# Woven stationary weights: two 128-column tiles side by side, element by element

## What is computed

```python
for l in range(DEPTH):                                   # first_block
    h = rms_norm(x, g_mix[l])
    proj = h @ w_in[l]                                   # 1024 x 10052, split into branch inputs and gates
    ...
    merged = gates[0] * (ya @ w_oa) + gates[1] * (yb @ w_ob) + gates[2] * (yc @ w_oc) + gates[3] * (yd @ w_od)
    x = x + merged @ w_merge[l]
    h2 = rms_norm(x, g_ffn[l])
    gt = causal_dwconv(h2 @ w_ffn_gate[l], ffn_conv_w[l])
    x = x + (silu(gt) * (h2 @ w_ffn_up[l])) @ w_ffn_down[l]
for l in range(DEPTH):                                   # second_block
    proj = rmsnorm(x, norm_w[l]) @ w_in[l]
    ...
    x = x + concat([y_mla, y_gdn, y_moba]) @ w_out[l]
```

## Time and profile before

| what | value |
|---|---|
| median of the runs shown (2: 1377.38 and 1378.05) | 1377.72 us |
| span of the profiled execution, first to last instruction | 1369.2 us |
| median less that span | 8.5 us |
| TensorE, matmuls busy / weight loads busy | 1345.0 / 1265.4 us |
| VectorE busy | 1040.0 us |
| ScalarE busy | 750.9 us |
| mean granted TensorE clock | 0.996 of full speed |

### The profile page before, as it was taken

How to read it: one execution, slowest core, us unless ns; L and a number is a source line. 1 busy time by engine, 2 the same in 40 slices (tenths; PEclk the granted TensorE clock), 3 DMA queues, 4 the chain that set the end, 5 groups by cost and what they waited for, 6 DMA issues and landing times. The chain is left out here.

```text
span 1369.2 us, 26498 instructions
## 1 busy us (share of the span) xinstructions
PE 1345.0 (98%) x10828; PEld 1265.4 (92%) x10828; DVE 1040.0 (76%) x1781; ACT 750.9 (55%) x1157; POOL 46.3 (3%) x48
## 2 busy tenths in 40 slices
PE   8999999999999999999999999999999999999998
PEld 8899999998999989899999999999989899888996
DVE  6999898677766666999897767766778746777565
ACT  6544656556444455544557545544558546576363
POOL 0000000000000000000000000000000110001100
PEclk9999999999999999999999999999999999999999
DMA  8565444564665465645364555555553324353231
GB/s 289 177 207 178 131 154 160 180 215 155 197 202 185 139 230 163 215 155 185 97 204 159 187 187 172 198 185 191 178 186 124 120 64 137 100 174 109 78 102 69
DMA packets 108992, 223.77 MB, mean 163 GB/s; under 512 B 6180, under 2 KB 17700, under 8 KB 108872
## 3 DMA queue, kind: packets, MB, share of 16 engines
q1 hardware_dynamic: 106736, 219.12, 48.2%
q10 hardware_dynamic: 2136, 2.96, 0.7%
HBM read 221.01 MB, written 1.06 MB: 162 GB/s over the span
## 5 line engine op out<-in xcount | busy, mean ns | idle before, releaser
L1755 DVE TENSOR_TENSOR wlo<-ring,whi 128x1024 fp32r<-128x1024 f32 (+3 forms) x430 | 498.1, 1180 | 182.7 <-ACT whi L1173 152.7
L1173 ACT ACTIVATE whi<-ring 128x1024 fp32r<-128x1024 f32 (+3 forms) x430 | 433.2, 1026 | 361.8 <-PE bank L499 228.7
L499 PE MATMUL bank<-hhi,whi 128*128 128x256 f32 x2016 | 278.8, 280 | 6.0 <-ACT sgb L1431 3.9
L508 PE MATMUL bank<-hhi,wlo 128*128 128x256 f32 x2016 | 280.3, 281 | 0.0
L499 PE MATMUL bank<-hlo,whi 128*128 128x256 f32 x2016 | 275.3, 278 | 0.0
L499 PEld LDWEIGHTS bank<-hhi,whi 128*128 128x128 f32 x2016 | 253.1, 189 | 9.5 <-ACT sgb L1431 4.3
L508 PEld LDWEIGHTS bank<-hhi,wlo 128*128 128x128 f32 x2016 | 252.6, 189 | 3.7 <-issue 2.6
L499 PEld LDWEIGHTS bank<-hlo,whi 128*128 128x128 f32 x2016 | 251.6, 189 | 0.0
L469 PE MATMUL bank<-w 64*64 64x64 f32 (+5 forms) x1376 | 101.7, 249 | 1.5 <-DMA w<-in_flip 0.9
L1935 DVE SCALAR_TENSOR_TENSOR w<-w,par 128x256 f32<-128x256 f32 x240 | 98.0, 478 | 0.0
L521 PE MATMUL bank<-whi,hhi 128*128 128x512 f32 (+2 forms) x256 | 96.6, 379 | 0.0
(11 more groups left out here) (309 smaller groups left out, 1535.5 us busy)
## 6 DMA issues: line engine op xcount, KB each, us to landing
ring<-in_w_in SPq DMA_DIRECT2D x100, 1024.0 KB, 5.1
ring<-in_w_ffn_down SPq DMA_DIRECT2D x22, 1024.0 KB, 5.1
ring<-in_w_ffn_gate SPq DMA_DIRECT2D x20, 1024.0 KB, 5.1
ring<-in_w_ffn_up SPq DMA_DIRECT2D x20, 1024.0 KB, 5.1
ring<-in_w_merge SPq DMA_DIRECT2D x8, 1024.0 KB, 5.1
ring<-in_w_out SPq DMA_DIRECT2D x8, 1024.0 KB, 5.0
ring<-in_w_oc SPq DMA_DIRECT2D x4, 1024.0 KB, 5.3
ring<-in_w_od SPq DMA_DIRECT2D x4, 1024.0 KB, 5.2
```

The lines of the kernel that those rows point to most:

```text
L499: done = e.matmul(o, wh[:, k, cols(u)], s_[:, k0 + k, :], stop=False, skip_group_check=True, start=opens and k == 0 and s_ is sh and u % 2 ...
L508: done = e.matmul(o, wl[:, k, cols(u)], sh[:, k0 + k, :], start=False, stop=closes, skip_group_check=True)
L1173: e.activation(part_of(whi, j), part_raw(j), ACT.Copy).then_inc(*up("hi.a"))
L1755: e.tensor_tensor(part_of(wlo, j), part_raw(j), part_of(whi, j), ALU.subtract).then_inc(*up("lo.v"))
```

## The change

Parts that `chans` uses are marked `woven`. In whi and wlo their columns are stored in pairs of tiles: for each k-row and each pair q of 128-column tiles, element i of the first tile, then element i of the second, and so on. Both splits write in this order (VectorE also reads whi in it) and read the ring as before. `chans` takes tile u as member u % 2 of pair u // 2, so its stationary operand has a step of two elements, 8 bytes. Parts for moving operands, `ba` and `cvg` stay as they were.

```diff
-        def load_k8(w, c0, c1):
+        def load_k8(w, c0, c1, weave=True):
...
-                load_k8(w, c0, c0 + (512 if n == 4 else n))
+                load_k8(w, c0, c0 + (512 if n == 4 else n), kind == "chans")
...
-                    load_k8(w, c0, c1)
+                    load_k8(w, c0, c1, name not in ("m0", "cvg"))
...
+        def weave_of(buf, j):
+            return part_of(buf, j).rearrange("p k (q i s) -> p (k q) s i", s=2, i=P)
+
+        def split_of(buf, j):
+            return weave_of(buf, j) if woven[j] else part_of(buf, j)
+
+        def split_raw(j):
+            raw = part_raw(j)
+            return raw.rearrange("p k (q s i) -> p (k q) s i", s=2, i=P) if woven[j] else raw
...
-                wh, wl = part_of(whi, j), part_of(wlo, j)
+                wh, wl = weave_of(whi, j), weave_of(wlo, j)
...
-                            done = e.matmul(o, wh[:, k, cols(u)], s_[:, k0 + k, :], stop=False, skip_group_check=True,
+                            done = e.matmul(o, wh[:, k * nq + u // 2, u % 2], s_[:, k0 + k, :], stop=False, skip_group_check=True,
...
-                        done = e.matmul(o, wl[:, k, cols(u)], sh[:, k0 + k, :], start=False, stop=closes,
+                        done = e.matmul(o, wl[:, k * nq + u // 2, u % 2], sh[:, k0 + k, :], start=False, stop=closes,
...
-                e.activation(part_of(whi, j), part_raw(j), ACT.Copy).then_inc(*up("hi.a"))
+                e.activation(split_of(whi, j), split_raw(j), ACT.Copy).then_inc(*up("hi.a"))
...
-                e.tensor_tensor(part_of(wlo, j), part_raw(j), part_of(whi, j), ALU.subtract).then_inc(*up("lo.v"))
+                e.tensor_tensor(split_of(wlo, j), split_raw(j), split_of(whi, j), ALU.subtract).then_inc(*up("lo.v"))
```

More of the change, by code:

```diff
@@ L378, in build, with load @@
         mask1 = cst[:, zo:zo + S]
-        loads, parts = [], []
-        def load(src, cuts):
+        loads, parts, woven = [], [], []
+        def load(src, cuts, weave=False):
             for c in cuts:
                 parts.append((len(loads),) + c)
+                woven.append(weave)
             assert src.shape[1] * src.shape[2] <= SLOT
             loads.append((src, src.shape[1], src.shape[2]))
-        def load_k8(w, c0, c1):
+        def load_k8(w, c0, c1, weave=True):
             for k in (0, 4):
-                load(w[:, k:k + 4, c0:c1], [(0, 2, 0, c1 - c0), (2, 4, 0, c1 - c0)])
+                load(w[:, k:k + 4, c0:c1], [(0, 2, 0, c1 - c0), (2, 4, 0, c1 - c0)], weave)
         def load_wide(w, k):
@@ L401, in build @@
             w = by_k(a["w_in"][l])
-            for _, _, n, c0 in MIX_IN:
-                load_k8(w, c0, c0 + (512 if n == 4 else n))
+            for _, kind, n, c0 in MIX_IN:
+                load_k8(w, c0, c0 + (512 if n == 4 else n), kind == "chans")
             for _, bi, name, _ in BRANCHES:
@@ L408, in build @@
                     load_k8(w, c0, c0 + 512)
-                    load(wo[:, :, 512 * hf:512 * hf + 512], [(0, 2, 0, 512), (2, 4, 0, 512)])
+                    load(wo[:, :, 512 * hf:512 * hf + 512], [(0, 2, 0, 512), (2, 4, 0, 512)], True)
             for i in range(4):
@@ L484, in chans @@
             def chans(j, held, n, src, k0, opens, closes, mid=None, normed=None):
-                wh, wl = part_of(whi, j), part_of(wlo, j)
+                wh, wl = weave_of(whi, j), weave_of(wlo, j)
                 sh, sl = src
-                kn = wh.shape[1]
+                kn, nq = 2, n // 2
                 e.wait_ge(SEM["hi.a"], j + 1)
```

## The result

| | before | after |
|---|---|---|
| median of the runs | 1377.72 us | 1402.74 us (2 runs, 1402.15 and 1403.34) |
| span of the profiled execution | 1369.2 us | 1400.4 us |
| ratio after / before | | 1.0189, 95% interval 1.0163 to 1.0215 |

Slower, by 25.0 us in the medians and 31.2 us in the spans. The forecast was 1369 us, with a range up to 1398. The two differences are unlike because the span of before lies 8.5 us under its median and that of after 2.3 us under its own. Every other kernel's profiled execution took 1.7 to 1.9 us more than its span, so the profiled execution of before took about 1371 us (an estimate) and was faster than either of the two in the table. On the chips of the experiments, where the kernel before ran beside the others, its medians are 1371.65 to 1373.67; against those the change costs 29 to 31 us.

The account below looks back on a forecast made before the run. TensorE was taken as the bound, number of products times their distance. Loads -9 us and splits zero took the span from 1369.2 to 1360, and the median from 1377.7 to 1368.7, say 1369 us; range 1334 to 1398.

Parts of the forecast that it names:

- What bounds the kernel: TensorE, busy 1345.0 of 1369.2 us with waits of at most 3.9 us: number of products times their start-to-start distance.
- The floor: For 256-column products, 113.3 ns is the moving columns streaming by themselves, not the loading of 128 columns.
- Loads: TensorE's loads of woven tiles: the longer distance goes away across 6816 products, taken as 9 us saved.
- the longer distance: 117.7 ns between 256-column products in the mixing stage against 113.3 in feed-forward; the 4.4 ns surplus comes once per tile loaded.
- the third: Rival on TensorE's loads: woven loads touch twice the memory lines and always meet the stream; +17 us, 1395; chance 0.11.
- its mark: Expected timeline sign of the third: all groups of eight at 1.10 us and weight loads longer than 0.19 us.
- The first rival: TensorE's two distances are a phase that the load's step does not touch; nothing moves, 1377.7 us; chance 0.24.
- The two rules: Trainium skill passages: by the read-port one time stays 1377.7; by the cacheline one neither splits nor loads pay anything.
- Splits: ScalarE's whi and VectorE's wlo writes (1063 and 1226 ns): taken as zero change, at most a doubling, +1.07 us each.
- The size of the verdict: Whole-kernel chances against a 2% threshold, 27.6 us: faster 0.15, slower 0.11, within 0.74.

Follow-up runs that it names:

- the bench: Separate kernel without the reference's computation: sets of 64 back-to-back products varying load step, moving width and tile size; 256 columns with full unit-step tiles took 120.0 ns by the starts.
- e2_writes: Kernel after, with woven writes kept but stationary tiles loaded at unit step; median 1374.01 us, ratio 1.0011 to the kernel before.
- e9_unit_112: Kernel before, with both weight buffers moved up 80 bytes, so tokens lie 112 bytes past weights modulo 256; 1404.80 us, ratio 1.0237 to the kernel before.
- e10_woven_80: Kernel after, with both weight buffers moved up 112 bytes, so tokens lie 80 bytes past weights modulo 256; 1417.83 us, ratio 1.0334 to the kernel before.

## Why the prediction was wrong, step by step

- **What bounds the kernel** held: the number of products times their distance, with no wait in between. The whole change of time is a change of that distance.
- **The floor** held: 113.3 ns is the 256 moving columns (32-column tiles at unit step: (7.4 - 0.277) / 63 = 113.1). The 8-column tiles of the bench have 113.6 at an 8-byte step and, for no reason that a run shows, 116.7 at unit step, both by the starts.
- **The step that failed is the term "Loads", -9 us.** It measured +31 us. I took the surplus of the longer distance to be a meeting of load and stream (the runs bear that out: it comes and goes with the addresses of the two, and with the size of the tile), and then let a step of 8 bytes take it away, on no more than that the order of the load changes. In place of it the runs showed two things. The stepped load takes longer by itself, 117.8 ns against 111.5, because it touches 64 lines of 16 bytes and not 32; no product can follow the last sooner than that, which is at least (117.8 - 115.2) x 6816 = +17.7 us. And a stepped load holds up the stream more than one of unit step does, also where it has time to spare (233.4 against 227.1 ns with 512 moving columns). In the kernel the distance is 120.0, (120.0 - 117.8) x 6816 = +15 us above the load alone. The sum, 32.7, is the span's growth within 1.5 us, but the two parts are an accounting: no run has the one without the other in the kernel.
- **The rivals.** The right one was the third, "every woven load touches twice the memory lines", at a chance of 0.11. Half of its mark was there (loads longer than 0.19 us, no group at 1.07; but the groups read 1.12 and not 1.10), and it was priced with the longest distance that the trace had, 117.7, so it gave +17 and 1395 where +31 was due. The step that mis-sized it is "even a load 5% slower would put every product at 117.7 or so": a load 5.6% slower puts it at 120 at these addresses. The range ended at 1398 because of that. A distance that no row shows can lie beyond the longest that rows show.
- **The first rival**, that the two distances are a phase which the step does not touch, is half right: at one set of addresses and unit step both exist (192 bytes in the table). But the step does touch it.
- **The two rules.** The Trainium skill, "TensorE: Matmul & The Clock Gate", the step on loading the stationary operand in Part 2, has two independent read ports and so no change. The runs disagree: 64 bytes of padding between the operands' buffers turn 113.3 or 117.7 into 120.0 ns with unit steps in both, and beside a stepped load the stream of 512 columns slows from 227.1 to 233.4. The Trainium skill, "SBUF — State Buffer", Door 1, the note on cachelines, says that two accesses per 16-byte line keep full bandwidth. The runs confirm the 16-byte line and nearly the rule: one and a third accesses per line cost 175.6 ns, one 233.4, two 117.8. But two are not quite four, 117.8 against 111.5, and in a kernel whose loads have 1 ns of room that is at least half of the loss. For the moving operand the rule fails by a factor of two: at two accesses per line 256 columns take 230 ns.
- **Splits** held: zero on VectorE (1226 to 1228 ns), and the 69 ns more on ScalarE lie in its idle time, as e2_writes shows (+0.1%). The last sentence of that part has the order reversed: the splits run up to four parts ahead of TensorE, not TensorE ahead of them. Nothing hung on it, since no split grew where it counted.
- **The size of the verdict.** The chances gave 0.11 to slower by over 2%; the result is 1.9% with an interval of 1.6 to 2.2, so these runs do not say on which side of the 2% it lies; that it is slower they do say.

What stays open: what in the two addresses decides (the difference modulo 256 bytes counts; e9_unit_112 and e10_woven_80 show that it is not all, and whether the rest is the place of the weights within 64 bytes was not tested by itself), how a stepped load holds up the stream, and what switches the kernel before between 113.3 and 117.7 with unchanged operands.

## What to carry to other kernels

Where loads of stationary tiles and the stream of moving columns are nearly as long as each other, keep both at unit step: with two elements in each 16-byte line instead of four a load took 6% longer here, with one it took twice as long. When buffers are moved, added or padded, look at the start distances of the products again, since an allocation that has nothing to do with them can change them by 6%. And try a layout change at more than one start of the other operand: the weaving cost some 29 us with the tokens 192 bytes past the weights, and against unit steps at 0 bytes it cost nothing.

## What was not expected of the hardware

- A load of 128 float32r elements per partition goes by 16-byte lines, about 1.82 ns each, once it touches 64 or more; at unit step it takes 111.5 ns for 32 lines. A stepped load slows the stream beside it even when it has time to spare: 512 moving columns take 233.4 ns in place of 227.1. A moving operand of 256 columns with an 8-byte step takes 230 ns in place of 113 to 120.
- With unit steps in both operands the distance of two 256-column products is anything from 113.3 to 123.5 ns (in two parts 129), by where the two operands lie, and the four pairs of starts 256 bytes apart that were run at unit step agree. At whole-kernel size, 64 bytes of padding are worth 2.1%.
- ScalarE's copy with an 8-byte output step is 6% slower (1132 against 1063 ns per 1024 elements); VectorE's subtraction with an 8-byte step in its output and in one input is not.
